# A two-layer block on one core: the first projection in unequal steps of contraction rows, x loaded in column quarters and turned tile by tile

## The reference, cut to what matters

```python
cond = silu(c)                                   # (1, 1024)
mod = cond @ ada_w[0] + ada_b[0]                 # (1, 3072)
shift, scale, gate = split(mod, 3)
h = x * (1 + scale) + shift                      # (512, 1024)
proj = h @ w_in                                  # w_in (1024, 5120)
u, v, z_a, x_b, z_b = split(proj, [1024, 2048, 3072, 4096])
```

## Time and profile before

| | |
|---|---|
| median of 3 runs | 1871.25 us (1869.6 to 1872.79) |
| the profiled execution | 1872.83 us |
| its span, first to last instruction | 1870.7 us |
| TensorE busy | 1806.8 us, 97% |
| VectorE, ScalarE, GpSimd busy | 43%, 40%, 42% |
| mean DMA rate over the span | 102 GB/s |
| DMA rate in the first fortieth (46.8 us) | 319 GB/s |

### The profile page before, as it was taken

The page is one execution under the profiler, slowest core; times in us unless marked ns, Lnnn a source line. Parts: engine busy times, 40 slices in busy tenths (PEclk is TensorE's granted clock), DMA queues, the critical chain, the costliest instruction groups (busy, mean ns, idle before and its releaser), DMA issues.

```text
span 1870.7 us, 24002 instructions
## 1 busy us (share of the span) xinstructions
PE 1806.8 (97%) x8798; PEld 1493.3 (80%) x8798; DVE 799.8 (43%) x1388; ACT 746.1 (40%) x1043; POOL 790.7 (42%) x992
## 2 busy tenths in 40 slices
PE   6999999989999999899999999999998999999998
PEld 5788888777888787888888888888865788888886
DVE  5775776476767634523241111103578341111102
ACT  3423331355565633322343443314456453443212
POOL 0374455453101253266335555353433135555351
PEclk9999999999999999999999999999999999999999
DMA  9543565221212142233233333323211133433321
GB/s 319 169 135 90 152 201 203 95 60 50 60 49 60 45 143 71 79 102 113 90 91 96 106 90 114 122 91 104 92 46 45 46 91 91 111 90 90 121 93 68
DMA packets 209320, 190.94 MB, mean 102 GB/s; under 512 B 10475, under 2 KB 189538, under 8 KB 209250
## 3 DMA queue, kind: packets, MB, share of 16 engines
q1 hardware_dynamic: 208608, 189.69, 32.6%
q10 hardware_dynamic: 642, 0.29, 0.1%
HBM read 187.86 MB, written 2.10 MB: 102 GB/s over the span
## 4 chain that ended last, share of the span: by engine, by line
PE 86%; DVE 5%; ACT 3%; POOL 3%; issue 2%; DMA 1%; SPq 0%; POOLq 0%; ACTq 0%; DVEq 0%
PE PS L1821 27%; PE PS L1823 26%; PE PS L1822 26%; POOL w_low L639 2%; PE PS L2177 1%; ACT w_high L743 1%; PE PS L1950 1%; PE PS L2208 1%; PE PS L2368 1%; POOL w_low L677 1%; DMA ada_raw<-in_ada_w 1%; PE PS L2356 1%; PE PS L2200 0%; DVE soft L1776 0%; DVE probs L1774 0%
## 5 line engine op out<-in xcount | busy, mean ns | idle before, releaser
L639 POOL TENSOR_TENSOR w_low<-w_raw,w_high 128x256 fp32r<-128x256 f32 x905 | 703.3, 813 | 835.2 <-ACT w_high L743 835.2
L1821 PE MATMUL PS<-h_high,w_high 128*128 128x512 f32 (+1 forms) x1488 | 560.8, 377 | 15.4 <-DVE h_low L1454 7.0
L1822 PE MATMUL PS<-h_low,w_high 128*128 128x512 f32 (+1 forms) x1488 | 553.7, 372 | 0.0
L1823 PE MATMUL PS<-h_high,w_low 128*128 128x512 f32 (+1 forms) x1488 | 553.7, 372 | 0.0
L743 ACT ACTIVATE w_high<-w_raw 128x2048 fp32r<-128x2048 f32 (+2 forms) x150 | 280.2, 1868 | 679.9 <-PE PS L1823 665.1
L1821 PEld LDWEIGHTS PS<-h_high,w_high 128*128 128x128 f32 x1488 | 281.9, 189 | 68.4 <-DVE h_low L1454 8.3
L1823 PEld LDWEIGHTS PS<-h_high,w_low 128*128 128x128 f32 x1488 | 281.7, 189 | 49.2
L1822 PEld LDWEIGHTS PS<-h_low,w_high 128*128 128x128 f32 x1488 | 282.1, 190 | 45.4 <-issue 0.7
L1363 DVE TENSOR_TENSOR gate_buf<-gate_buf,PS 128x512 f32<-128x512 f32 x44 | 30.3, 688 | 334.9 <-ACT gate_buf L876 334.3
L1183 DVE TENSOR_TENSOR w_low<-w_raw,w_high 128x2048 fp32r<-128x2048 f32 (+1 forms) x15 | 33.3, 2220 | 317.0 <-ACT w_high L743 317.0
L1821 PE MATMUL PS<-w_high,ff_high 128*128 128x512 f32 x352 | 137.2, 390 | 0.1
(11 more groups left out here) (310 smaller groups left out, 2580.0 us busy)
## 6 DMA issues: line engine op xcount, KB each, us to landing
w_raw<-in_f_gate_up SPq DMA_DIRECT2D x88, 512.0 KB, 4.9
w_raw<-in_f_down SPq DMA_DIRECT2D x40, 512.0 KB, 4.2
w_raw<-in_e_w_in SPq DMA_DIRECT2D x32, 512.0 KB, 5.1
gains<-in_ada_w SPq DMA_DIRECT2D x16, 1024.0 KB, 5.2
w_raw<-in_a_w_in SPq DMA_DIRECT2D x24, 512.0 KB, 4.5
w_raw<-in_o_w_in SPq DMA_DIRECT2D x20, 512.0 KB, 4.5
ada_raw<-in_ada_w SPq DMA_DIRECT2D x8, 1024.0 KB, 13.5
w_raw<-in_e_w_out SPq DMA_DIRECT2D x16, 512.0 KB, 6.4
```

Of the source, the lines that this page charges most:

```text
L639: ins = nc.gpsimd.tensor_tensor(WL[s][:, piece], raw[s][:, piece], WH[s][:, piece].bitcast(F32), ALU.subtract)
L1821: mm(dst, lh, rh, start=first, stop=False, skip_group_check=True)
L1822: mm(dst, lh, rl, start=False, stop=False, skip_group_check=True)
L1823: return mm(dst, ll, rh, start=False, stop=last, skip_group_check=True)
```

## The change

The first stage is cut and ordered anew; the arithmetic of the result stays.

- x_b has six column tiles (`XB_TILES` = 6) in the k-outer part, in five steps: k tile 0, k tile 1, then two tiles each (`STEPS`). A chunk of a single k tile has 768 columns, one of two has 1536. The last two column tiles come as two chunks of 128 columns by all k (`XB_AT` = 5 and 6), so "front" has 8 entries in each slot and z_b starts with chunk 7.
- The first two pieces of ada_w hold 128 columns of shift and 128 of scale for one k tile each (`mixed_ada`). Piece 0 comes in two halves of k, with two DMAs of 256 KB for each. Pieces 2 to 7 are as before, under new numbers.
- x is loaded in four quarters of 256 columns, in between the pieces. Each k tile is turned alone, into bank 6 only, and modulated out of PSUM; `x_turned` and its copies are gone. The turns of tiles 1 to 7 stand among the matmuls.
- 30 turns of the identity into bank 5, which nothing reads, stand ahead of column 0, and 12 more behind the turn of tile 0.
- VectorE: piece 0 alone, step 0, piece 1, step 1, then two pieces for each step; in the later steps the first half of the next piece's terms is done ahead of or behind the low parts of h.
- ScalarE issues the load of gmlp_ws behind the modulation of tile 0, not at the start.

```diff
-    ("front", 7, (2, 2)),
+    ("front", 8, (2, 2)),
...
+STEPS = ((0,), (1,), (2, 3), (4, 5), (6, 7))
+XB_TILES = 6
+FRONT_SIZE = [len(kts) * XB_DEEP for kts in STEPS] + [K * P] * 2 + [CHUNK] * 9
+XB_AT, ZB_AT, V_AT, POOL_AT = 5, 7, 11, 15
...
 # SyncE
+            mixed_ada(0, slice(0, K // 2), ada_half)
+            mixed_ada(0, slice(K // 2, K), ada_full[0])
+            load_x(0)
             load_xb(0)
-            for t in range(T):
-                sp.dma_start(x[:, t, :], a["x"][t * P:(t + 1) * P, :]).then_inc(x_in[t], 16)
+            mixed_ada(1, slice(0, K), ada_full[1])
+            load_xb(1)
             for j in range(1, 4):
                 first_ada(2 * j)
                 first_ada(2 * j + 1)
-                load_xb(j)
+                load_x(j)
+                load_xb(j + 1)
+            load_xb_last(0)
+            load_xb_last(1)
...
 # ScalarE
+            def modulated(kt):
+                act.wait_ge(mod_ready, STEP_OF[kt] + 1)
                 act.wait_ge(xt_tr, kt + 1)
+                if kt >= 4:
+                    act.wait_ge(hx_low, kt - 3)
+                nact(h_tmp[kt % 4], PS[:, 6, :], ACT.Identity, scale=mod[:, K + kt:K + kt + 1], bias=mod[:, kt:kt + 1]).then_inc(xt_free, 1)
+                act.wait_ge(xt_free, kt + 1)
                 nact(hH[:, kt, :], h_tmp[kt % 4], ACT.Copy).then_inc(hx_high, 1)
+            for j, kts in enumerate(STEPS):
                 front_high(j)
+                for kt in kts:
+                    modulated(kt)
+                if j == 0:
+                    act.dma_start(ws_sb, a["gmlp_ws"].rearrange("h t s -> t h s")).then_inc(rest_in, 16)
+            front_high(XB_AT)
+            front_high(XB_AT + 1)
...
 # VectorE
+            first_terms(0, head)
+            first_terms(0, rest_k)
+            mod_keep(0)
+            split_low("front", 0, 0, FRONT_SIZE[0])
+            mod_low(0)
+            first_terms(1, all_k)
+            mod_keep(1)
+            split_low("front", 0, 1, FRONT_SIZE[1])
+            mod_low(1)
+            for j in range(2, len(STEPS)):
+                n = 2 * j - 2
+                first_terms(n, all_k if j == 2 else rest_k)
+                first_terms(n + 1, all_k)
+                split_low("front", j // 2, j % 2, FRONT_SIZE[j])
+                mod_keep(j)
+                if j + 1 < len(STEPS) and j > 2:
+                    first_terms(n + 2, head)
+                for kt in STEPS[j]:
+                    mod_low(kt)
+                if j == 2:
+                    first_terms(n + 2, head)
...
 # TensorE
+            idle_turns(30)
             first_column(0)
+            turn_x(0)
+            idle_turns(12)
...
+            xb_part(0, 0, 1)
+            turn_next(1)
+            xb_part(0, 1, 4)
+            first_column(1)
+            xb_part(0, 4, XB_TILES)
+            xb_part(1, 0, 2)
+            turn_next(2)
+            xb_part(1, 2, 3)
+            first_column(2)
+            xb_part(1, 3, XB_TILES)
+            first_column(3)
+            for j in range(2, len(STEPS)):
+                kt, n = STEPS[j][0], 2 * j
+                turn_next(kt + 1)
+                if j + 1 == len(STEPS):
+                    xb_part(kt, 0, XB_TILES)
+                    xb_part(kt + 1, 0, XB_TILES)
+                    continue
+                xb_part(kt, 0, 4)
+                first_column(n)
+                xb_part(kt, 4, XB_TILES)
+                xb_part(kt + 1, 0, 1)
+                turn_next(kt + 2)
+                xb_part(kt + 1, 1, 2)
+                first_column(n + 1)
+                xb_part(kt + 1, 2, XB_TILES)
+            for m in range(2):
+                front_split(XB_AT + m)
...
+                for k in range(K):
+                    ins = mm3(PS[:, XB_TILES + m, :], WH[s][:, c], WL[s][:, c], hH[:, k, :], hL[:, k, :], k == 0, k == K - 1)
```

More of the change, by code:

```diff
@@ L256, in program @@
         yb = dz("y_pool", 8192, [P, K, S])
[L257 removed]
+        ada_raw = [dz(f"ada_raw{n}", 2048 * n, [P, CHUNK]) for n in range(K)]
         ada_part = [dz(f"ada_part{n}", 16384 + 512 * n, [P, 2, 256]) for n in range(4)]
[L259 removed]
         h_tmp = [gains[:, m // 2, (m % 2) * S:(m % 2 + 1) * S] for m in range(4)]
@@ L699, in _ @@
                 if name == "front":
-                    for c in range(4, 2 * pairs):
+                    for c in range(XB_AT, 2 * pairs):
                         if c != ZB_AT:
@@ L839, in _ @@
             act.wait_ge(pool_ready, 1)
-            for f in range(K):
+            for f in range(XB_TILES):
+                xb_out(f)
+            front_high(ZB_AT)
+            for f in range(XB_TILES, K):
                 xb_out(f)
@@ L1163, in _, with first_terms @@
             dve.wait_ge(csil_ready, 1)
[L1164 to L1167, removed]
+            def first_terms(n, ks):
+                part = ada_part[n % 4]
+                if n == 0:
+                    dve.wait_ge(*((ada_half, 32) if ks.start == 0 else (ada_full[0], 32)))
+                elif ks.start == 0:
+                    dve.wait_ge(ada_full[n], 32 if n == 1 else 16)
+                if n >= 4 and ks.start == 0:
                     dve.wait_ge(ada_done, n - 3)
-                w = ada_raw[c][:, :].rearrange("p (k n) -> p k n", n=256)
-                for k in range(K):
+                w = ada_raw[n][:, :].rearrange("p (k c) -> p k c", c=256)
+                for k in range(ks.start, ks.stop):
                     dst, ck = part[:, k % 2, :], csil[:, k:k + 1]
@@ L1993, in front_split, with xb_part @@
                 pe.wait_ge(w_split[c % 2], B.split[c % 2] + c // 2 + 1)
-            for kt in range(K):
-                j, s = kt // 2, kt // 2 % 2
-                if kt % 2 == 0:
-                    front_split(j)
-                pe.wait_ge(hx_low, kt + 1)
-                for f in range(XB_TILES):
-                    if kt == 0:
-                        pe.wait_ge(xt_free, f + 1)
-                    c = slice((kt % 2) * XB_DEEP + f * P, (kt % 2) * XB_DEEP + (f + 1) * P)
+            def xb_part(kt, first, last):
+                j = STEP_OF[kt]
+                s, at_ = j % 2, (kt - STEPS[j][0]) * XB_DEEP
+                if first == 0:
+                    if kt == STEPS[j][0]:
+                        front_split(j)
+                    pe.wait_ge(hx_low, kt + 1)
+                for f in range(first, last):
+                    c = slice(at_ + f * P, at_ + (f + 1) * P)
                     ins = mm3(PS[:, f, :], WH[s][:, c], WL[s][:, c], hH[:, kt, :], hL[:, kt, :], kt == 0, kt == K - 1)
```

131 lines of the change are left out of this document (52 added, 79 removed).

## The result

| | before | after |
|---|---|---|
| median of 16 runs each | 1872.21 us (1869.6 to 1874.25) | 1875.92 us (1873.47 to 1878.97) |
| ratio, with 95% interval | | 1.0021 (1.0015 to 1.0028) |
| profiled execution, and its span | 1872.83, 1870.7 us | 1874.74, 1872.8 us |

A forecast was written before the change was run, and what follows sets the result against it. TensorE, busy 97% of the span, was taken as the bound, the first zb chunk's start as deciding. Earlier start, moved work and removed stalls gave -6.6 us, new waits +7.65, so +1.05: 1872.4 us, range 1867.7 to 1875.9.

The forecast's parts named there:

- The gain at M0: Start of the kernel: first main matmul (k tile 0) at 14.5 us against 23.35, that is -8.85 us.
- the loss behind it: Behind the first main matmul: new TensorE stalls sum to 7.65 us, moved work adds 3.15 and one column 0.9.
- the wait before column 6: First stage: TensorE waits from 47.3 us for VectorE's terms 6, which end at 48.4; 1.15 us.
- the handover from f6 to zb: From the ring slot freed by f6, ScalarE's split, GpSimd's half and handover take 7.12 us to the first zb chunk.
- ScalarE is not held at its issue: Rival denied here: issuing the ws load under a full queue holds ScalarE; price +5, about 1876 us; chance 0.10.
- three signs of being wrong: First main matmul off by over 1.5 us, ScalarE's issue row over 4 us, or the stretch behind 80 us changing length.
- a fixed cost in series: First ada_w megabyte as four 256 KB pieces: fixed DMA cost paid serially, whole about 6 us slower; chance 2%.
- The tail: Tiles f6, f7 into zb: zb starts at 77.4 us against 76.32; VectorE's later terms cost 0 to +1, taken 0.
- M1: First matmul of k tile 1: at 21.45 us, behind a stall of 1.3 us.
- landing of xb 2: Transfer of the x_b chunk whose split precedes tile 2's mod: lands at 26.3 us, bounds 24.3 to 28.
- M2: First matmul of k tile 2: at 32.15 us, stall 2.4, as mod waits in VectorE's order behind xb 2's split.
- half rate: Rival: TensorE falls to its lower clock level in the gaps; +2.2 us, 1874.5; chance 0.13 together with late first matmul.

The follow-up runs named there:

- ada_first: Changed kernel with SyncE issuing the load for ada_terms(0) ahead of the first zb load; 1872.8 us, ratio 1.0008 to the kernel before.
- after_again: The changed kernel run once more, unedited, for the scatter from trace to trace; 1878.0 us, ratio 1.0033 to the kernel before.
- no_idle: Changed kernel without its 42 turns of the identity; 1876.2 us, ratio 1.0030 to the kernel before.
- fit26: fill_fit with 26 instead of 36 identity turns behind the turn of tile 0; 1875.3 us, ratio 1.0019 to the kernel before.
- fill: Changed kernel with 36 identity turns instead of 12 behind tile 0's turn, and zero products around tile 3's turn; 1879.1 us, ratio 1.0041 to the kernel before.
- long_runs: ada_first with the first two ada_w pieces read in runs of 256 columns, result not the reference's; 1872.8 us, ratio 1.0007 to the kernel before.
- terms_early: ada_first with VectorE's first half of the terms of piece 2 moved ahead of tile 1's modulation; 1875.0 us, ratio 1.0016 to the kernel before.
- fill_fit: ada_first with 36 identity turns behind tile 0's turn and gap-fitted zero products around tile 3's turn and ahead of columns 4 and 6; 1875.2 us, ratio 1.0017.
- before_idle: Kernel before with 30 turns of the identity ahead of column 0 and nothing else; 1872.2 us, ratio 1.0000.

## Why the prediction was wrong, step by step

**What was right.** The gain at M0 and the loss behind it (7.6 us won, and 11.4 lost by zb), the wait before column 6 (1.15 forecast, 1.14 measured), the handover from f6 to zb (forecast 7.12 us; ScalarE's split at 73.03 to zb at 80.09 is 7.06, in part by luck, since VectorE's half was now the last to end and not GpSimd's), the pace of 0.227 us in the steady part, and that ScalarE is not held at its issue, which refutes that rival. ScalarE's DMA issue in the timeline of after:

```profile
14.24 0.41 ACTq L803 DMA_DIRECT2D gains<-in_gmlp_ws  x1
```

The forecast named three signs of being wrong. M0 was off by 1.2 us, less than the 1.5 named, and ScalarE's issue row was short; but the stretch behind 80 us did change its length, by 1.2 us from zb to sv.

Four pieces of 256 KB did not pay a fixed cost in series: the halves of piece 0 let VectorE start at 6.28 and 8.47 us (forecast 7.0 and 8.8). The rule that was weighed there, from the Trainium skill (DMA: Bandwidth & Descriptors, Bandwidth), to batch DMAs to a megabyte, is not borne out by these rows as a cost of each piece.

**The step that failed: "The tail".** It said that VectorE's terms come up to 4 us later, "0 to +1 us, I take 0", and the forecast let everything behind zb "move as a block". VectorE's terms came at 73.55, 7.6 us later than before (65.98): the load was issued 5.0 us later (65.79 against 60.83) and took 2.6 us longer to land, right behind the zb chunk. I had followed the delay only to the next matmul. The term that I took as 0 measures 1.4 us in the changed kernel and 2.2 us in the kernel before, and most of it falls 47 us behind the place where I looked, through VectorE's sums, ScalarE's order and GpSimd's eight parts. Both directions were run: undone, both waits shrink to what they were before; added alone, both appear. (That ada_first's median, 1872.8, lies near the forecast is luck: its zb was 1.8 us behind the forecast's.)

This step is not the whole miss. At sv the forecast was a lag of 1.1 us and the trace has 5.0. Of the 3.9 us between them the tail is 1.4 (0.2 at zb, 1.2 ahead of v), the late landing of xb 2 is 1.3, half pace ahead of M1 is 0.5 and the stretch from M2 to the last matmul of f7 0.6; the rest is rounding.

**Terms that were mis-sized.** M0 was 14.5 by the sum and 15.73 (14.55 in the second trace). The landing of xb 2 was 26.3 by the sum; its split began between 26.1 and 27.6 in after, after_again, ada_first, no_idle and fit26. M1 was 24.09 against 21.45: 1.2 us of it are M0's, the rest is half pace (fill, with the same M0 at full pace: 22.46). M2 was 34.06 against 32.15.

**The rival "half rate" came true, and cost less than its price.** It was forecast at +2.2 us; in the changed kernel it cost about 0.5, all ahead of M2 (1.4 in after_again, by the same reckoning from the landing). Before M2 three things end within about 1 us of each other in most traces: the landing of xb 2 plus 5.9 us (fit26, 27.25 to 33.18), VectorE's order of terms, split and modulation (after: busy from 23.86 to 31.41 without a pause, as it was let go late by M1 at half pace), and the column on TensorE (after_again: 30.38, where TensorE was at half pace from 26.6 on). Taking away one leaves the others; ada_first to fit26 takes away half pace (0.2 us at M2, with a landing 0.25 us later), no_idle had an early landing (26.12) and half pace and came at 34.66, and only long_runs, with an early landing and full pace ahead of M2, reached 31.76. This also explains what the sum got right for a wrong reason: the stall at column 4 (1.4 forecast) is absent in after and 1.54 us in fill, the wait for x quarter 1 (1.4) is absent in after and 1.30 in after_again. A slow TensorE hides them.

**Slips in the working.** The 9.41 us of the chain end at 11.99, so they are the second piece's and not the first's, and 27.69 us scaled from 8.1 to 6.8 MB gives 24.1, not 24.3. Neither moves the sum by more than 0.2 us.

**What stays open.** Medians follow the lag at sv only roughly (correlation 0.93 over the 16 kernels): ada_first, terms_early, fit26 and fill_fit lag by 2.5 to 3.0 us and have 1872.8, 1875.0, 1875.3 and 1875.2 us. A part of the difference lies behind all that the change touches. From sv to the end the traces took 1686.4 us in before, 1683.5 and 1685.8 in after and after_again, and 1682.2 in ada_first. Slow stretches occur there too, near the same places in two traces of the changed kernel (375, 410, 755 and 1435 us) but of different lengths, and the mean granted clock over an execution goes with its time: a common fit within the kernels, over all runs, gives 0.95 us for 0.001 of clock. fit26 had a mean of 0.9932, before 0.9953, ada_first 0.9946. But correcting all times to one clock leaves the correlation with sv at 0.93 and moves single kernels far (against before: after +1.9, ada_first +0.8, long_runs -0.4, before_idle -2.4 us with a lag of +0.9), so it doesn't settle what separates these kernels. Whether a start decides where the later slow stretches fall was not settled either. Effects under 2 us are therefore read from the traces here, and that ada_first, long_runs and before differ in time isn't shown. Nothing that was run beats the kernel before by more than its interval.

## What to carry to other kernels

When a load is put behind a wait, cost every load behind it in the same queue, and follow each one through the engines that work in order until a wait absorbs it; the bill can come two stages later. An earlier start is worth only as much as the latest of the suppliers allows: 7.6 us here were worth nothing, since the transfer of xb 2, VectorE's order and TensorE's column end close together and each of them holds M2 by itself. Work that only keeps an engine busy must fit the gap that it fills, and it pays only where that engine is the limit.

## What the hardware showed beside

- The granted clock reads 1.00 from the start, while 30 turns took 6.37 us (0.21 us each) and 12 took 1.47 (0.12): until its first change is recorded the pace has to be read from the distance of starts.
- How early a queued chunk lands varies between executions of the same program: in two traces of the changed kernel the first xb chunk's split began at 12.69 and 11.51 us and that of xb 2 at 27.60 and 26.58.
- GpSimd's subtraction of four parts took 2.82 us with VectorE idle, and 3.56 and 4.73 with VectorE at work beside it. GpSimd's timeline in the changed kernel, where VectorE waited until 73.55 and was at its terms from then on:

```profile
68.73 2.82 POOL L658 TENSOR_TENSOR w_low<-w_raw,w_high 128x256 fp32r<-128x256 f32 x4 [4.06 <-ACT w_high L762]
...
75.03 3.56 POOL L726 TENSOR_TENSOR w_low<-w_raw,w_high 128x256 fp32r<-128x256 f32 x4 [3.47 <-ACT w_high L762]
```

and in ada_first, where VectorE was at its half and the pooling sums:

```profile
74.33 4.73 POOL L726 TENSOR_TENSOR w_low<-w_raw,w_high 128x256 fp32r<-128x256 f32 x4 [2.90 <-ACT w_high L762]
```

So GpSimd was faster beside a late VectorE, and a part of the loss at zb was paid back. The Trainium skill (GPSIMD Engine Reference, Specifications) says that GpSimd shares its way to SBUF with VectorE and contends with VectorE's instructions that have two inputs in SBUF; the trace agrees, and shows that VectorE pays too: beside GpSimd its terms started 0.88 us apart in place of 0.40.
